# The last stage of a hybrid block: tile order 1, 0, 2 to 7, a first read in two halves, constant products on TensorE, and the norm weight multiplied ahead of the root

## The reference

```python
h = rms_norm(x, pre_norm_ffn[l]) * (1.0 + sc2) + sh2
y = hierarchical_moe(h, ...)      # top-1 group, then top-2 experts in it, of 32
x = x + g2 * rms_norm(y, post_norm_ffn[l])

def rms_norm(x, g):
    return x * lax.rsqrt(jnp.mean(x * x, axis=-1, keepdims=True) + EPS) * g
```

## Time and profile before

| | |
|---|---|
| median of 3 runs | 1033.19 us (1032.94 to 1033.48) |
| the profiled execution | 1034.08 us |
| its span | 1032.3 us |
| TensorE busy | 965.2 us, 93% |
| VectorE busy | 521.3 us, 50% |
| ScalarE busy | 302.2 us, 29% |
| GpSimd busy | 218.1 us, 21% |

### The profile page before, as it was taken

One profiled execution on the slowest core, in us unless ns is written; L12 is line 12 of the kernel. 1 busy time (PEld: TensorE's weight loads), 2 busy tenths in 40 slices (PEclk: granted clock), 3 DMA queues, 4 the chain that ended last, 5 costly groups with the idle time before them and its releaser, 6 DMA issues. The chain is left out here.

```text
span 1032.3 us, 14924 instructions
## 1 busy us (share of the span) xinstructions
PE 965.2 (93%) x5439; PEld 576.1 (56%) x5439; DVE 521.3 (50%) x959; ACT 302.2 (29%) x585; POOL 218.1 (21%) x268
## 2 busy tenths in 40 slices
PE   6999999999989999989999999899999998999946
PEld 4444444444556556658566665596555554555512
DVE  3356346444765555556578776572333332333327
ACT  3310002222553434432222222113333332333313
POOL 2200000222600830003333312021222211222003
PEclk9999999999999999999999999999999998999968
DMA  9986323000000000004012112995999999998557
GB/s 336 373 330 231 134 112 51 0 1 0 7 1 1 1 2 1 1 19 187 21 62 79 66 62 107 411 386 194 395 417 413 403 410 402 413 415 322 197 212 287
DMA packets 51823, 192.53 MB, mean 187 GB/s; under 512 B 15322, under 2 KB 20514, under 8 KB 36258
## 3 DMA queue, kind: packets, MB, share of 16 engines
q1 hardware_dynamic: 43396, 173.10, 43.3%
q0 software_dynamic: 7056, 18.36, 4.6%
q10 hardware_dynamic: 1296, 0.07, 0.1%
HBM read 174.21 MB, written 24.64 MB: 193 GB/s over the span
## 5 line engine op out<-in xcount | busy, mean ns | idle before, releaser
L1623 PE MATMUL PS<-ring,xg_T 128*64 x736 | 165.5, 384 | 7.2 <-ACT near_gu L1800 6.3
L1623 PE MATMUL PS<-near_gu,xg_T 128*64 128x256 f32 x736 | 165.5, 384 | 0.0
L1623 PEld LDWEIGHTS PS<-ring,xg_T 128*64 128x64 f32 x736 | 101.8, 139 | 68.6 <-issue 22.8
L1504 PE MATMUL PS<-w_out_sb,cat_T 128*128 128x512 f32 x256 | 118.0, 602 | 3.2 <-DVE y_sc L1945 2.8
L1013 PE MATMUL PS<-hT,w_x 128*128 128x512 f32 x256 | 111.6, 594 | 0.0
L427 POOL TENSOR_SCALAR rstd<-stat 128x1 f32<-128x1 f32 (+1 forms) x48 | 21.2, 441 | 382.6 <-ACT junk L611 187.7
L1623 PEld LDWEIGHTS PS<-near_gu,xg_T 128*64 128x64 f32 x736 | 101.8, 139 | 0.0
L1649 PE MATMUL PS<-ring,hid_T 128*64 x184 | 83.8, 598 | 0.4 <-DVE hid_T L2161 0.4
L1649 PE MATMUL PS<-near_dn,hid_T 128*64 128x512 f32 x184 | 83.9, 598 | 0.0
L2152 DVE TENSOR_TENSOR hid<-PS,hid_s 128x128 f32<-128x128 f32 x46 | 11.3, 286 | 138.7 <-PE PS L1623 138.7
L1013 PEld LDWEIGHTS PS<-hT,w_x 128*128 128x128 f32 x256 | 48.1, 190 | 58.9 <-issue 58.2
(11 more groups left out here) (336 smaller groups left out, 1564.4 us busy)
## 6 DMA issues: line engine op xcount, KB each, us to landing
ring<-in_w_gate_dram SPq DMA_DIRECT2D x32, 1024.0 KB
ring<-in_w_up_dram SPq DMA_DIRECT2D x32, 1024.0 KB
ring<-in_w_down_dram SPq DMA_DIRECT2D x32, 1024.0 KB
ada_later<-in_ada_w_dram SPq DMA_DIRECT2D x16, 1024.0 KB, 4.8
ada_first<-in_ada_w_dram SPq DMA_DIRECT2D x16, 512.0 KB, 11.0
y_g<-y_rows SPq DMA_DIRECT2D x8, 1024.0 KB, 11.7
x_in<-in_x_dram SPq DMA_DIRECT2D x8, 512.0 KB, 9.5
w_x<-in_w_in_dram SPq DMA_DIRECT2D x4, 1024.0 KB, 15.2
```

The source lines that it names most:

```text
L1504: last = pe.matmul(BANK[6 + j], cat_T[t % 2][:, k, :], w_out_sb[:, k, j * HALF:(j + 1) * HALF], start=(k == 0), stop=(k == KC - 1))
L1623: last = pe.matmul(BANK[2 + s_][rows_, 0:FF], xg_T[b][:, k, rows_], gu[u][:, s_, k, :], start=(k == 0), stop=(k == KC - 1))
```

## The change

Four edits in the last stage:

1. **Order.** The tiles are taken in the order 1, 0, 2, 3, 4, 5, 6, 7 on all engines. Tile 0's first sum stays ahead of the loop; tile 4's `scaled` and `summed` now follow tile 2 in the loop.
2. **First read in halves.** Tile 1 is read by two DMAs of 512 columns of both rows each, with semaphores `yg_first` and `yg_loaded1`; TensorE waits for the first ahead of its first two products and for the second ahead of the other two.
3. **Constant products.** TensorE runs `busy(7, 46)` between its wait for `w_diag` and its wait for the first half.
4. **Norm weight ahead of the root.** VectorE multiplies the sum by G2 as soon as the tile is squared (`tensor_tensor`, waiting for `ysum_sq`), and after `rstd_done` does y * rstd + x2 in one `scalar_tensor_tensor`. VectorE's wait for the residual rows, `x2_back`, moves ahead of the loop.

```diff
+        ORDER = (1, 0, 2, 3, 4, 5, 6, 7)
@@ SP
                 sp.wait_ge(S["moe_stored"], 1)
-                for t in range(NT):
-                    sp.dma_start(y_g[t][:, :, :], y_rows[2 * t * P:2 * (t + 1) * P, :].rearrange("(p j) d -> p j d", j=2))\
-                        .then_inc(S[f"yg_loaded{t}"], 16)
-                for t in range(NT):
-                    sp.wait_ge(S["o_done"], t + 1)
+                for i, t in enumerate(ORDER):
+                    rows_t = y_rows[2 * t * P:2 * (t + 1) * P, :].rearrange("(p j) d -> p j d", j=2)
+                    if i == 0:
+                        sp.dma_start(y_g[t][:, :, 0:HALF], rows_t[:, :, 0:HALF]).then_inc(S["yg_first"], 16)
+                        sp.dma_start(y_g[t][:, :, HALF:], rows_t[:, :, HALF:]).then_inc(S[f"yg_loaded{t}"], 16)
+                    else:
+                        sp.dma_start(y_g[t][:, :, :], rows_t).then_inc(S[f"yg_loaded{t}"], 16)
+                for i, t in enumerate(ORDER):
+                    sp.wait_ge(S["o_done"], i + 1)
                     sp.dma_start(out[0, t * P:(t + 1) * P, :], y_sum[t][:, :]).then_inc(S["o_stored"], 16)
@@ GpSimd
-                for t in range(NT):
-                    inverse_root(pool, 7, t, S["ysum_sq"], t + 1)
+                for i, t in enumerate(ORDER):
+                    inverse_root(pool, 7, t, S["ysum_sq"], i + 1)
@@ TensorE
                 pe.wait_ge(S["w_diag"], 1)
+                busy(7, 46)
                 for n, t in enumerate(PE_TILES):
-                    pe.wait_ge(S[f"yg_loaded{t}"], 16)
                     if n >= 4:
-                        pe.wait_ge(S["o_scaled"], PE_TILES[n - 4] + 1)
+                        pe.wait_ge(S["o_scaled"], ORDER.index(PE_TILES[n - 4]) + 1)
                     for j in range(D // HALF):
+                        if n == 0 and j == 0:
+                            pe.wait_ge(S["yg_first"], 16)
+                        elif n == 0 or j == 0:
+                            pe.wait_ge(S[f"yg_loaded{t}"], 16)
                         for k in range(2):
@@ ScalarE
                 scaled(0)
-                for t in range(NT):
-                    if t + 1 < NT and t + 1 not in PE_TILES:
-                        scaled(t + 1)
+                for i, t in enumerate(ORDER):
                     if t in PE_TILES:
                         act.wait_ge(S["ysum_pe"], PE_TILES.index(t) + 1)
                     else:
-                        act.wait_ge(S["ysum_done"], t + 1 - on_pe(t))
-                    if t:
-                        act.wait_ge(S["ysum_sq"], t)
+                        act.wait_ge(S["ysum_done"], 1 + t // 4)
+                    if i:
+                        act.wait_ge(S["ysum_sq"], i)
                     act.activation(junk[:, :], pe_sum(t) if t in PE_TILES else y_sum[t][:, :], ACT.Square, scale=D ** -0.5,
                                    accum_out=stat[:, 7, t:t + 1]).then_inc(S["ysum_sq"], 1)
+                    if t == 2:
+                        scaled(4)
@@ VectorE
                 summed(0)
-                for t in range(NT):
-                    if t + 1 < NT and t + 1 not in PE_TILES:
-                        summed(t + 1)
+                dve.wait_ge(S["x2_back"], 16 * NT)
+                for i, t in enumerate(ORDER):
                     y = y_sum[t][:, :]
-                    dve.wait_ge(S["rstd_done"], 2 * NT + t + 1)
-                    dve.scalar_tensor_tensor(y, pe_sum(t) if t in PE_TILES else y, rstd[:, 7, t:t + 1], G2[:, :], ALU.mult, ALU.mult)\
-                        .then_inc(S["o_scaled"], 1)
-                    dve.wait_ge(S["o_scaled"], t + 1)
-                    if t == 0:
-                        dve.wait_ge(S["x2_back"], 16 * NT)
-                    dve.tensor_tensor(y, y, x2_all[:, t, :], ALU.add).then_inc(S["o_done"], 1)
+                    dve.wait_ge(S["ysum_sq"], i + 1)
+                    dve.tensor_tensor(y, pe_sum(t) if t in PE_TILES else y, G2[:, :], ALU.mult).then_inc(S["o_scaled"], 1)
+                    dve.wait_ge(S["o_scaled"], i + 1)
+                    dve.wait_ge(S["rstd_done"], 2 * NT + i + 1)
+                    dve.scalar_tensor_tensor(y, y, rstd[:, 7, t:t + 1], x2_all[:, t, :], ALU.mult, ALU.add)\
+                        .then_inc(S["o_done"], 1)
+                    if t == 2:
+                        summed(4)
```

More of the change, by code:

```diff
@@ L271, in hybrid_block @@
         BANK = [PS[:, i, :] for i in range(8)]
-        def on_pe(t):
-            return sum(1 for v in PE_TILES if v < t)
         def pe_sum(t):
@@ L299, in hybrid_block @@
             yg_loaded3 yg_loaded4 yg_loaded5 yg_loaded6 yg_loaded7 moe_stored w_diag ysum_pe
-            rstd_y rstd_yo rstd_x2 rank_early rev_made gate_done router_exp route_act ranks_done slots_done idx_done idx_read""".split()
+            rstd_y rstd_yo rstd_x2 rank_early rev_made gate_done yg_first router_exp route_act ranks_done slots_done idx_done idx_read""".split()
         EARLY = """x_loaded0 x_loaded1 win_x_loaded0 win_rest_loaded ada_loaded0 ada_loaded1 first_loaded2 ada_row_loaded
@@ L2205, in summed @@
                 def summed(t):
-                    dve.wait_ge(S["ya_scaled"], t + 1 - on_pe(t))
+                    dve.wait_ge(S["ya_scaled"], 1 + t // 4)
                     dve.scalar_tensor_tensor(y_sum[t][:, :], y_g[t][:, 1, :], wts[:, 1, t:t + 1],
```

## The result

The changed kernel takes 1035.15 us in the median of 18 runs, the kernel before 1033.07 in 18 runs beside it; the ratio is 1.0022, interval 1.0011 to 1.0032. It is slower by 2.1 us in the medians and by about 2.3 us (1.1 to 3.3) by the ratio, where 2.6 had been forecast (1035.8 against 1033.19). Single executions spread widely, 1032.3 to 1039.8 after and 1030.7 to 1035.3 before, so one profile of each is compared by its last stage alone, counted from the eviction of the last expert rows (VectorE's y_e, 986.98 before and 986.33 after) to VectorE's last end.

The account below looks back on a forecast made before the run. The last stage was taken as bound by TensorE up to 1013.7, then VectorE at 2.46 us a tile. Median 1033.19 plus 2.4 us, and half of 0.45 for the clock, gave 1035.8 us, range 1034.0 to 1037.2.

Parts of the forecast that it names:

- part 1: TensorE's 46 products behind w_diag: 12.9 us from 992.5, so tile 1's sums start at 1005.4, not 1000.09.
- The formula: Start of TensorE's tile 1 sums: 992.5 + 10.4 + 0.47 times the clock's return, taken as 5.3 us.
- rival 1: Not slower: TensorE's clock returns early in the products, after 3.4 instead of 5.3 us; 1034.3 to 1034.7 us; chance 0.33.
- the forecast's line: Boundary to rival 1: clock return of 4.6 us with one met root, 5.5 with none; 0.2% is 2.07 us.
- the sum: VectorE released on tile 1 at 1010.25, then never idle; ends at 1031.7 instead of 1029.29, +2.4 us.
- meeting with GpSimd: GpSimd's root falls due beside VectorE operations with two SBUF inputs; VectorE waits 0.45 us; one of two counted.
- part 4: GpSimd's roots of tiles 0 and 4 blocked by VectorE: one 0.45 us wait counted, bounds 0 and 0.9.
- part 2: Order and halved first read: half lands near 996.3, gains nothing; bandwidth loss 0 to 1 us, counted 0.
- the price of the order: VectorE finished tile 0 in the gap before tile 1; now tile 0's 2.46 us come behind tile 1.
- part 3: Norm weight ahead of root: VectorE's pair stays 2.46 us; GpSimd's root hides behind a 1.23 us product, gaining once.

Follow-up runs that it names:

- e2: Kernel before plus only the 46 constant products behind the wait for w_diag; ratio to the kernel before 1.0030 (1.0016 to 1.0044).
- e1: Changed kernel without its 46 constant products; order, halves and norm weight stay; ratio to the kernel before 0.9989 (0.9976 to 1.0002).
- e10: Changed kernel with two lines exchanged, so the 46 products stand ahead of the wait for w_diag; ratio to the kernel before 0.9990 (0.9965 to 1.0015).
- e3: Changed kernel with 34 products ahead of the wait for w_diag and none behind it; ratio to the kernel before 0.9990 (0.9975 to 1.0006).
- e12: Changed kernel with 44 products ahead of the wait for w_diag and a whole first read, run again; ratio to the kernel before 0.9948 (0.9926 to 0.9971).
- e5: Changed kernel without products and with tile 1 read whole by one DMA; ratio to the kernel before 0.9980 (0.9964 to 0.9995).
- e6: Kernel before with the new tile order alone; ratio to the kernel before 0.9994 (0.9982 to 1.0005).
- e8: Changed kernel with 44 products ahead of the wait for w_diag and a whole first read; ratio to the kernel before 0.9952 (0.9937 to 0.9966).
- e9: Kernel before, old order, with norm weight ahead of the root and 50 products ahead of the w_diag wait; ratio to before 0.9972 (0.9960 to 0.9983).
- e4: Kernel before with only the norm weight multiplied ahead of the root; ratio to the kernel before 0.9997 (0.9978 to 1.0017).

## Why the prediction was right, point by point

**The products (part 1).** Shown, by e2, e1 and e10. The formula, 10.4 us plus 0.47 times the return, gives 12.05 us for the return of 3.5 us in this profile; 12.17 were measured. The size of the return, 5.3 us, was right partly by luck. It was the mean of 4.5, 5.2 and 6.2 us, but in the first two the clock was still full when TensorE restarted (at 462.52 and 656.32); it fell at 463.57 and 658.12 and stood at half for 3.4 us. Only the third is a restart at half clock:

```profile
463.50:463.75 0.25, 0.25 (x4) 0.25 (x3) 0.22 (x3) 0.00 (x0) 0.00 (x0) 0.63 3.36 852
658.00:658.25 0.25, 0.25 (x4) 0.25 (x4) 0.00 (x0) 0.00 (x0) 0.00 (x0) 0.75 1.18 492
```

Still, 5.3 us lies within the returns seen since (3.3, 3.3, 3.5, 4.3, 5.1, 6.0, 6.1 and the 6.2 of before); those with products behind the semaphore are 3.3, 3.5 and 6.1. The profiled execution is rival 1's case: its stage is 1.26 us longer than before, e2's 1.44. The medians are 2.1 us apart, which is the forecast's line between itself and rival 1 (2.07 us), and the interval of 1.1 to 3.3 us holds both. So the loss and its cause are shown, the choice between forecast and rival 1 is not.

The scatter of whole times goes with the clock, but this return is too small to make it. Each execution has its mean granted clock on record. The three fastest of the changed kernel (1032.3 to 1032.8 us) had 0.990 to 0.991, the three slowest (1037.7 to 1039.8) 0.983 to 0.985, and over all 18 the correlation is -0.85. A return that is 2.9 us longer lowers the mean by 0.0014 only and costs 1.4 us, so most of that difference in clock arose ahead of the last stage; which of clock and time drives the other is not shown.

**Tile 1 to the end (the sum).** VectorE's run from tile 1's square to the end was to be 21.45 us with one meeting with GpSimd; it is 1008.49 to 1029.90, 21.41. That run began 22.16 us after the eviction, where 23.27 had been forecast: 0.85 of the difference is the shorter return, 0.25 an earlier w_diag. The pair stays at 2.46 us, also with its product from PSUM (1.22).

**GpSimd (part 4).** One meeting, at tile 4, for 0.53 us (0.45 forecast). At tile 0 GpSimd's add, 0.03 us ahead of VectorE, slipped in and took 0.22; only the pow was stretched, to 1.44, and still came in time. In e1, e3, e10 and e12 the meeting at tile 0 did happen, 0.53 us again: there VectorE was 0.07 to 0.10 us ahead. The rule that was quoted from the Trainium skill (SBUF — State Buffer, "SBUF: two separate sides") is that the one that starts first holds the other off for a whole instruction. The trace agrees where VectorE came first (0.22 us became 1.26). That GpSimd, coming first, holds off VectorE doesn't show: VectorE's operation at 1009.75 took its usual 1.28 us beside the add.

**The read in halves (part 2).** This was mis-sized. The first half landed at 992.15 + 4.2 = 996.35, and the forecast 996.3 was met by luck, since this execution's stage began 0.65 us earlier. From its issue it took 4.2 us, where 3.5 had been assumed; whole first reads took 4.8 and 4.9 (e12, e5), so halving brought TensorE's data forward by some 0.6 us and not by 1.25. The line of the second half, and the last of its answer:

```profile
L1327 SPq DMA_DIRECT2D y_g<-y_rows x1: 608/608/608, 992.7 to 992.7; - x1
...
DMA to landing us min/median/max: 6.6/6.6/6.6
```

It landed at 992.74 + 6.6 = 999.3, 7.2 us after the first issue, so tile 1 was complete 2.4 us later than by one read. Tile 0 followed 2.6 us behind, at 1001.92, 15.6 us after the eviction and not 13.1: 2.5 us late, where 0 to 1 had been bounded. It did no harm only because the products covered it.

**The order (part 2).** "That is the price of the order" holds only behind the products, which made VectorE wait anyway. Without them (e6) no cost of the order shows, and with TensorE at full clock it gains (e8 against e9, by the profiles).

**The root (part 3).** In e4's profile it gains once, as forecast (1.3 us); the medians don't settle it. In the changed kernel GpSimd's root of tile 1 (1008.48 to 1009.36) lies beside VectorE's product (1008.49 to 1009.71), so the gain is in the run of 21.4 us.

## What to carry to other kernels

Filler work that shall keep an engine's clock up has to end when the data comes, and gives most when it starts while the clock is still up: count its time from the instruction in front of it in the stream, at the clock of that moment. Forty-six products nearly fitted the wait from the last expert product to the data; behind a semaphore 5.3 us into it they outlasted it by 7. Sixteen in that place ended 2 us after the first half and ahead of tile 0, and cost nothing that showed. And when an edit seems free since a slower one hides it, as the halved read did, price it again for the version without the slower one.

## What the runs showed of the hardware

Two reads of 512 KB in place of one of 1 MB, at the head of a queue of eight reads, delayed the next one by 1.1 to 3.3 us (tile 0 at 14.23 to 16.41 against 13.14, the mean of the four whole ones). In windows of the changed kernel (first issue at 992.15) the rate climbs slowly:

```profile
994.00:996.00 2.00, 2.00 (x15) 2.00 (x15) 0.00 (x0) 0.00 (x0) 0.00 (x0) 0.72 0.93 281
996.00:998.00 2.00, 2.00 (x20) 2.00 (x20) 0.00 (x0) 0.00 (x0) 0.00 (x0) 1.00 1.04 381
...
1002.00:1004.00 2.00, 2.00 (x18) 1.83 (x17) 0.89 (x1) 1.07 (x1) 0.00 (x0) 1.00 1.02 430
```

The same windows of e12 (first issue at 992.27), which reads tile 1 whole:

```profile
994.00:996.00 2.00, 2.00 (x20) 2.00 (x20) 0.00 (x0) 0.00 (x0) 0.00 (x0) 1.00 0.94 385
996.00:998.00 2.00, 1.64 (x11) 1.19 (x10) 0.00 (x0) 0.00 (x0) 0.00 (x0) 1.00 1.01 422
```

With the halves the DMA engines are as busy as without them (0.93 and 0.94, then 1.04 and 1.01) and move less, 281 and 381 GB/s against 385 and 422. The queue shows 2704 packets instead of 2304 in the stage for the same 12.58 MB. A whole read of a tile has 128 pieces of 8 KB, since the two expert rows of a token lie side by side in `y_rows`; in halves the same megabyte has 512 pieces of 2 KB. These 384 more, and 16 for one more semaphore, are the 400. So the shorter pieces are a likely cause, though no run here tells them from the second DMA itself; why the delay varies stays open.

In the eight kernels without early products the clock fell 2.2 to 5.4 us after TensorE's last expert product (988.95 against 986.73 in e6, 991.71 against 986.28 in the changed kernel), and once TensorE worked again the full clock came back after 3.3 to 6.2 us.
